# Inner RMS norms of a 2+2 layer network: the eight tiles of squares are added by TensorE products with ones, and no longer by VectorE

## The reference, cut to what matters

```
def rms_norm(x, g, eps=NORM_EPS):
    xf = x.astype(jnp.float32)
    y = xf * lax.rsqrt(jnp.mean(xf * xf, axis=-1, keepdims=True) + eps)
    return (y * g.astype(jnp.float32)).astype(x.dtype)
...
x = x + 0.5 * rms_norm(swiglu(rms_norm(x, g[0]), ffn_wgu[i, 0], ffn_wd[i, 0]), g[1])
h = rms_norm(x, g[2])
...   # mix: diff attention + RWKV in layer 0 ("even"), retention in layer 1 ("odd")
x = x + rms_norm(mix, g[3])
x = x + 0.5 * rms_norm(swiglu(rms_norm(x, g[4]), ffn_wgu[i, 1], ffn_wd[i, 1]), g[5])
```

## Time and profile before

| what | value |
|---|---|
| median of three runs | 3604.89 us |
| the profiled execution, its own time | 3607.89 us |
| its span, first to last instruction | 3606.0 us |
| TensorE busy | 3491.7 us, 97% of the span |
| VectorE busy | 1945.3 us, 54% |
| ScalarE busy | 1247.4 us, 35% |
| GpSimd busy | 446.5 us, 12% |
| mean granted TensorE clock | 0.99 of full |

### The profile page before, as it was taken

One profiled execution on the slowest core, in us unless ns is written; L12 is line 12 of the kernel. 1 busy time (PEld: TensorE's weight loads), 2 busy tenths in 40 slices (PEclk: granted clock), 3 DMA queues, 4 the chain that ended last, 5 costly groups with the idle time before them and its releaser, 6 DMA issues.

```text
span 3606.0 us, 47520 instructions
## 1 busy us (share of the span) xinstructions
PE 3491.7 (97%) x18803; PEld 2786.7 (77%) x18803; DVE 1945.3 (54%) x2695; ACT 1247.4 (35%) x1773; POOL 446.5 (12%) x358
## 2 busy tenths in 40 slices
PE   8999999999999999999988899999999999999998
PEld 6888888545888878887776688878888787778887
DVE  5655563465555555545666455456445534465555
ACT  5532232464422342224643332233222422242222
POOL 1320011010100021112023011111111000011111
PEclk9999999999999999999999999999999999999999
DMA  3332234100232322323100132222232222213231
GB/s 118 105 109 93 93 94 99 42 1 24 83 104 94 104 85 94 99 89 98 59 14 26 36 105 95 92 93 94 93 105 93 82 82 82 82 59 105 93 98 65
DMA packets 232546, 295.80 MB, mean 82 GB/s; under 512 B 21894, under 2 KB 201465, under 8 KB 232393
## 3 DMA queue, kind: packets, MB, share of 16 engines
q1 hardware_dynamic: 230864, 290.48, 25.2%
q0 software_dynamic: 1152, 3.05, 0.4%
q10 hardware_dynamic: 376, 0.12, 0.0%
HBM read 291.53 MB, written 2.10 MB: 81 GB/s over the span
## 4 chain that ended last, share of the span: by engine, by line
PE 88%; DVE 6%; ACT 3%; issue 2%; POOL 1%; DMA 0%; POOLq 0%; SPq 0%; DVEq 0%; ACTq 0%
PE bank L309 25%; PE bank L311 25%; PE bank L310 25%; POOL tmp L682 1%; PE bank L338 1%; PE bank L340 1%; PE bank L339 1%; ACT whi L299 1%; PE bank L2922 1%; DVE wlo L305 1%; PE bank L2431 1%; PE bank L1570 1%; PE bank L1485 1%; PE bank L1554 1%; PE bank L2912 0%
## 5 line engine op out<-in xcount | busy, mean ns | idle before, releaser
L309 PE MATMUL bank<-h_hi,whi 128*128 128x512 f32 x2780 | 1096.1, 394 | 33.5 <-DVE h_lo L741 10.0
L311 PE MATMUL bank<-h_hi,wlo 128*128 128x512 f32 x2780 | 1082.3, 389 | 0.0
L310 PE MATMUL bank<-h_lo,whi 128*128 128x512 f32 x2780 | 1081.7, 389 | 0.0
L299 ACT ACTIVATE whi<-raw 128x2048 fp32r<-128x2048 f32 x267 | 510.3, 1912 | 1254.6 <-PE bank L311 1202.6
L305 DVE TENSOR_TENSOR wlo<-raw,whi 128x2048 fp32r<-128x2048 f32 x267 | 614.3, 2301 | 321.5 <-ACT whi L299 321.5
L309 PEld LDWEIGHTS bank<-h_hi,whi 128*128 128x128 f32 x2780 | 523.1, 188 | 162.3 <-issue 37.9
L310 PEld LDWEIGHTS bank<-h_lo,whi 128*128 128x128 f32 x2780 | 523.5, 188 | 108.5 <-issue 3.6
L311 PEld LDWEIGHTS bank<-h_hi,wlo 128*128 128x128 f32 x2780 | 523.0, 188 | 108.9
L309 PE MATMUL bank<-u_hi,whi 128*128 128x512 f32 x1408 | 548.9, 390 | 4.6 <-DVE arena L2998 2.4
L311 PE MATMUL bank<-u_hi,wlo 128*128 128x512 f32 x1408 | 547.8, 389 | 0.0
L310 PE MATMUL bank<-u_lo,whi 128*128 128x512 f32 x1408 | 547.8, 389 | 0.0
(11 more groups left out here) (436 smaller groups left out, 3102.3 us busy)
## 6 DMA issues: line engine op xcount, KB each, us to landing
raw<-in_ffn_wgu SPq DMA_DIRECT2D x88, 1024.0 KB, 5.0
raw<-in_ffn_wd SPq DMA_DIRECT2D x44, 1024.0 KB, 5.0
raw<-in_mlp_w_up SPq DMA_DIRECT2D x32, 1024.0 KB, 5.3
raw<-in_mlp_w_down SPq DMA_DIRECT2D x32, 1024.0 KB, 5.0
raw<-in_odd_w_in SPq DMA_DIRECT2D x24, 1024.0 KB, 5.2
raw<-in_even_w_in SPq DMA_DIRECT2D x13, 1024.0 KB, 5.3
raw<-in_rg_w_in SPq DMA_DIRECT2D x8, 1024.0 KB, 5.8
raw<-in_odd_w_out SPq DMA_DIRECT2D x8, 1024.0 KB, 5.1
```

The lines of the kernel that those rows point to most:

```text
L299: e.activation(whi[:, n % 2, :], raw[:, n % 2, :], ACT.Copy).then_inc(hi_ready, 1)
L309: pe.matmul(o, w_hi, r_hi, start=first, stop=False)
L310: pe.matmul(o, w_hi, r_lo, start=False, stop=False)
L311: return pe.matmul(o, w_lo, r_hi, start=False, stop=last)
```

## The change

For the six inner norms with an owed norm ahead of them, VectorE's seven additions go. TensorE's `pe_sum` waits for the eighth square, multiplies each of the eight tiles by ones and adds them up in PSUM; the token sums are taken over eight tiles too. GpSimd waits for `n_sum` in place of `n_add`. The count of `n_add` for the plain norms is renumbered (`plain_no`), which changes no instruction.

```
         def pool_norm(e, stage):
             if PLAN[stage][1] is not None:
                 pool_owed(e, stage)
-                e.wait_ge(n_add, 7 * j + 7)
+                e.wait_ge(n_sum, j + 1)
                 return
...
         def pe_sum(pe, stage):
             j = norm_no[stage - 1]
-            pe.wait_ge(n_add, 7 * j + 7)
+            if PLAN[stage - 1][1] is not None:
+                pe.wait_ge(n_sq, KT * j + KT)
+                if PLAN[stage][0] in TOKENS:
+                    for q in range(QT):
+                        for k in range(KT):
+                            pe.matmul(NTOK[:, q:q + 1], fsum[:, k, q * P:q * P + P], ones[:, 0:1], start=k == 0, stop=k == KT - 1)
+                for k in range(KT):
+                    ins = pe.matmul(NSUM, ones[:, :], fsum[:, k, :], start=k == 0, stop=k == KT - 1)
+                ins.then_inc(n_sum, 1)
+                return
+            pe.wait_ge(n_add, 7 * plain_no[stage - 1] + 7)
...
         def dve_norm(e, stage, chain):
                 dve_lo_piece(e, stage, 3)
-                j = norm_no[stage]
-                for k in range(1, KT):
-                    e.wait_ge(n_sq, KT * j + k + 1)
-                    if k > 1:
-                        e.wait_ge(n_add, 7 * j + k - 1)
-                    e.tensor_tensor(acc, fsum[:, 0, :] if k == 1 else acc, fsum[:, k, :], ALU.add).then_inc(n_add, 1)
-                    if k == 4:
-                        dve_lo(e, ends[stage - 1] + 2)
+                dve_lo(e, ends[stage - 1] + 2)
                 dve_lo(e, ends[stage - 1] + 3)
                 return
```

More of the change, by code:

```diff
@@ L267, in build @@
         norm_no = {i: sum(s_[0] == "norm" for s_ in PLAN[:i]) for i in range(len(PLAN))}
+        plain_no = {i: sum(s_[0] == "norm" and s_[1] is None for s_ in PLAN[:i]) for i in range(len(PLAN))}
         owed_no = {i: sum(s_[0] in ("norm", "post") and s_[1] is not None for s_ in PLAN[:i]) for i in range(len(PLAN))}
@@ L626, in act_norm @@
                     act_high_tile(e, stage, k)
-                    square(e, x, k, n_add, 7 * j, n_sq)
+                    square(e, x, k, n_add, 7 * plain_no[stage], n_sq)
                 act_hi(e, ends[stage - 1] + 1)
@@ L650, in act_norm @@
                             final(e, stage, k2)
-                            square(e, x, k2, n_add, 7 * j, n_sq)
+                            square(e, x, k2, n_add, 7 * plain_no[stage], n_sq)
                 act_hi(e, ends[stage - 1] + 1)
@@ L700, in pool_norm @@
                 if k > 1:
-                    e.wait_ge(n_add, 7 * j + k - 1)
+                    e.wait_ge(n_add, 7 * plain_no[stage] + k - 1)
                 e.tensor_tensor(acc, tmp[:, 4, :] if k == 1 else acc, tmp[:, 4 + k % 3, :], ALU.add).then_inc(n_add, 1)
```

## The result

| | before | after |
|---|---|---|
| median, same chip | 3607.82 us (4 runs) | 3669.74 us (4 runs, 3662.93 to 3672.10) |
| ratio, 95% interval | | 1.0172, 1.0154 to 1.0190 |
| profiled execution, span | 3606.0 us | 3668.0 us |

Slower by 62 us, as forecast in sign, but 10 us more than the 51.7 of the sum, and outside the range. The span grew by 62.0 us too, so the two profiled executions can be set against each other.

A forecast was written before the change was run, and what follows sets the result against it. TensorE, busy 97% of the span, was taken to bound the kernel. 0 + 36.1 + 12.3 + 3.3 = 51.7 us on the profiled 3607.9 gave 3659.6, forecast as 3657 for a median run, range 3648 to 3665.

The forecast's parts named there:

- the 51.7 of the sum: Whole kernel: 0 for the removal, 36.1 wide, 12.3 narrow and 3.3 for GpSimd's lateness, 51.7 us slower.
- the removal: Six inner norms: dropping VectorE's 42 additions, 29 us of its time, gives 0, bounds 0 to 1.9 us.
- Wide products: TensorE's sum at six places: seven more products of 0.86 us each, 6.0 us a place, 36.1 us in all.
- Narrow products: Token sums in even and odd: 28 more products at each, 0.22 us apiece, 12.3 us in all.
- GpSimd's delay: GpSimd starts 4.25 us later in s00, paid but for 0.4 us of slack; hidden in the other stages.
- The wait in s00: Ahead of the first down product in s00, TensorE waits 3.3 us for VectorE's `wlo`, through late GpSimd.
- The rule of the Trainium skill: VectorE with two SBUF inputs slows GpSimd's SBUF reads: s00 wait 3.3 us with it, 3.9 without.
- They stand in TensorE's order ... and so nothing hides them: Wide products at six places stand between products following without a gap, so all 36.1 us is on the path.
- A: Rival: GpSimd's delay in s00 is hidden, leaving the sums alone, 48.4 us, time 3653; chance 18%.
- B: Rival: GpSimd's delay costs more than once, in s00's second group or even's tables; 57 us, time 3662; chance 14%.
- C: Rival: in the sums, wide products repeating the same weights run cheaper, 0.43 us each; time 3639; chance 2%.
- D: Rival: not slower, as VectorE's 29 us bound the six norms or TensorE's later waits vanish; 3605; chance 1%.

The follow-up runs named there:

- b_noadds: Kernel before without VectorE's 42 additions, sums over the last tile of squares alone, GpSimd waiting for the eighth square; ratio 1.0013.
- a_both: Changed kernel with GpSimd waiting for the eighth square and narrow products in four groups of 8 with 2 wide ones between; 3656.73 us, ratio 1.0147.
- a_inter: Changed kernel with the even and odd stages' products reordered into four groups of 8 narrow and 2 wide; 3659.68 us, ratio 1.0158.
- b_pool_sum: Kernel before with one wait altered: GpSimd waits for TensorE's sum and not VectorE's last addition; ratio 1.0023.
- a_pool_sq: Changed kernel with one wait altered: GpSimd waits for the eighth square and not TensorE's sum; 3663.52 us, ratio 1.0161.
- b_narrow: Kernel before with each of the four narrow products in even and odd done eight times, wide sum left single; 3623.64 us, single run.
- b_r: Kernel before with the owed sums and the inner sum as reduced products, their inputs written in that form; 3598.16 us, ratio 0.9976.

## Why the prediction was wrong, by its own steps

**Right.** Nothing came of the removal: b_noadds. Wide products at 0.86, 6.0 us a place: s01 +5.99, and s00, s01, s11 of a_both. Narrow products at 0.22 as long as the clock is full: +12.26 in a_inter. GpSimd's delay is paid in s00 and in no other stage: b_pool_sum. In the kernel after GpSimd started its tables 1.3 us behind the start of the last wide product (1308.8 by the pace of 0.86), for a forecast of 1.1.

**A size off.** The wait in s00 was 3.73, not 3.3: GpSimd's step L1928 took 1.94 us for the 1.78 I had worked out of a stretched row, and GpSimd started 0.2 us later against TensorE than I had set. The rule of the Trainium skill ("SBUF — State Buffer", "Who interferes with whom") held in kind: away from VectorE's `wlo` the step was shorter than the 2.35 beside it. But it took 1.94 in a_pool_sq with VectorE idle too, so the stretch was 0.41 us and not the 0.57 for which the two had overlapped, and 3.73 lies between the 3.3 with the rule and the 3.9 without it.

**The step that failed** is the sentence "They stand in TensorE's order ... and so nothing hides them" with its companion "TensorE alone so gets 36.1 + 12.3 = 48.4 us", and the stall priced at its own length alone. Both price TensorE's new work at the pace that the rows of before show at full clock, and take it for given that the clock stays. It did not, at three places: in the new pause of s00 (3.0 us lost behind it), within the narrow row of even (5.1 us) and of odd (3.4 us). That is 11.5 us. With 1.9 us ahead of the first cut, 0.4 for the wait, and 3.4 given back by the clock in even's recurrence, this is 10.4 for the 10.3 us that were missing. a_pool_sq and a_inter each take one of these causes away and the half clock goes with it; b_pool_sum and b_narrow put each into the kernel before and the half clock comes.

The Trainium skill ("TensorE: Matmul & The Clock Gate", "What's actually happening") states that the clock of the array is set by how busy it has been. The trace agrees for s00, where the clock fell within the 3.73 us in which TensorE did nothing. In the narrow rows the trace does not show it: the profile has TensorE busy all the time, and the clock fell too. By that page the half clock behind the pause should have been a rival of mine; I named none on the clock.

The trace of before had the hint. At five of the six places TensorE pauses for 2.4 to 2.8 us ahead of the owed norm's first product (0.4 ahead of s01), and behind two of the five the clock was at half, behind the others not. The first products ahead of s00, after 2.45 us of idle time, and ahead of s11, kernel before:

```profile
1266.95 0.70 PE L709 MATMUL bank<-tmp,ones 128*128 128x256 f32 x2 [2.45 <-POOL tmp L682]
...
3215.39 1.22 PE L709 MATMUL bank<-tmp,ones 128*128 128x256 f32 x2 [2.75 <-POOL tmp L682]
```

That costs some 1.7 us a place and lands on different norms in different executions: before on those ahead of odd and s11, after on those ahead of s10 and odd. It is why s10 shows +7.67 and s11 +4.33, which cancel.

The rivals: A (no wait in s00) is refuted by the trace. B was wrong in its mechanism though its time of 3662 was nearer: s00 has no second wait, and in b_pool_sum, where GpSimd is late too, even is only 0.1 us longer. C is refuted by the 16 records over 6.87 us of a sum, D by the ratio.

Not settled: how the executions come to differ in where the clock falls, in even's recurrence and behind the owed norms, and for how long it stays down behind the pause of s00. No run here varies that alone. Nor does a run vary the columns of the narrow products alone: that they bring the clock down is shown, by a_inter and b_narrow; what in them does it is not.

## What to carry to other kernels

Work moved from an engine with slack to the one that bounds the kernel costs its full length there: count it in that engine's time, and ask who waited for the engine that is now done later, here GpSimd with 0.4 us of slack. Price every new pause and every row of thin products on TensorE twice, once at full and once at half clock, and put thin products between full ones, which gave back 5.0 us in even and 3.3 in odd. And ask for the form of a product first: the same eight wide products cost 1.8 us in the reduced form for 6.9, and b_r, which changes only that, is the one version here that is faster than the kernel before.

## What the runs showed of the hardware that I had not expected

- A row of one-column float32 products brings TensorE's granted clock from 2.4 to 1.2 GHz while the profile shows it busy all the time: the clock fell 3.6 to 5.4 us behind the first of them, in even and odd, of the kernel after and of b_narrow. Eight such products (1.7 us) between pairs of 512-column ones left it at 2.4 in a_inter, and so did a row of 62-column ones of 7 us in the kernel before.
- In a pause of 3.7 us the clock fell in each of the three executions seen (after, a_inter, b_pool_sum), with one of 2.4 to 2.8 us in some norms only. Behind the pause of 3.7 us 6.2, 2.9 and 5.7 us of products ran at half speed.
- The even stage, with many waits of 1 us, takes 411 to 417 us with the same work, mostly by the clock.
